# The state-space recurrence regrouped into chunks of four tokens, with its small matrices built on the chip

## The reference

```python
def s5_mixer(h, h0, lam_re, lam_im, log_dt, b_re, b_im, c_re, c_im, d_skip, w_glu):
    lam = lax.complex(lam_re, lam_im); dt = jnp.exp(log_dt)[:, None]
    a_bar = jnp.exp(lam * dt)
    b_bar = ((a_bar - 1.0) / lam)[..., None] * lax.complex(b_re, b_im)
    u = h.reshape(Bt, S, SSM_GROUPS, SSM_P)                # 64 groups of 16 channels
    bu = jnp.einsum('bsgp,gnp->bsgn', u, b_bar)            # 64 complex states a group
    bu = bu.at[:, 0].add(a_bar[None] * h0)
    _, states = lax.associative_scan(combine, (a, bu), axis=1)   # s_t = a s_(t-1) + bu_t
    y = jnp.real(jnp.einsum('bsgn,gpn->bsgp', states, c_mat)) + d_skip * u
    z = y @ w_glu
    return z[..., :D] * jax.nn.sigmoid(z[..., D:]), last_state
```

## Time and profile before

| | us |
|---|---|
| median of three runs | 2583.43 |
| the profiled execution, its time | 2582.37 |
| the profiled execution, its span | 2580.6 |
| TensorE busy | 2400.8 (93%) |
| VectorE busy | 1625.4 (63%) |
| ScalarE busy | 963.7 (37%) |
| GpSimd busy | 802.7 (31%) |

### The profile page before, as it was taken

The page is one execution under the profiler, slowest core; times in us unless marked ns, Lnnn a source line. Parts: engine busy times, 40 slices in busy tenths (PEclk is TensorE's granted clock), DMA queues, the critical chain, the costliest instruction groups (busy, mean ns, idle before and its releaser), DMA issues.

```text
span 2580.6 us, 48876 instructions
## 1 busy us (share of the span) xinstructions
PE 2400.8 (93%) x17574; PEld 2207.2 (86%) x17574; DVE 1625.4 (63%) x3405; ACT 963.7 (37%) x1664; POOL 802.7 (31%) x580
## 2 busy tenths in 40 slices
PE   4689789999999999999968988899999999999998
PEld 1344679999999999999958666699999999999998
DVE  6999736978899733333345442279788996333333
ACT  1122225444444344444423332254444344444443
POOL 0278736790000022222245300268700001222222
PEclk6699999999999999999989988899999999999999
DMA  8555234443333444444453463344433334444443
GB/s 307 185 211 180 78 133 140 164 145 130 123 130 128 151 163 165 169 163 164 167 218 111 175 255 138 125 139 160 142 131 124 129 130 157 163 165 168 163 163 140
DMA packets 105467, 405.81 MB, mean 157 GB/s; under 512 B 12864, under 2 KB 13248, under 8 KB 102176
## 3 DMA queue, kind: packets, MB, share of 16 engines
q1 hardware_dynamic: 98064, 357.74, 39.8%
q10 hardware_dynamic: 7312, 46.93, 4.7%
HBM read 395.48 MB, written 9.14 MB: 157 GB/s over the span
## 4 chain that ended last, share of the span: by engine, by line
PE 62%; issue 17%; DVE 10%; POOL 9%; ACTq 1%; ACT 1%; DMA 0%; POOLq 0%; DVEq 0%
PE ps L1239 11%; PE ps L1231 10%; PE ps L1235 10%; POOL ring_lo L1827 7%; PE ps L1211 6%; PE ps L1210 6%; PE ps L1214 6%; PE ps L1198 5%; DVE big L1548 2%; POOL ring_lo L1834 1%; PE ps L1109 1%; PE ps L1105 1%; PE ps L1106 1%; DVE big L1540 1%; PE ps L706 1%
## 5 line engine op out<-in xcount | busy, mean ns | idle before, releaser
L330 ACT ACTIVATE wt_hi<-ring 128x1024 fp32r<-128x1024 f32 x564 | 593.7, 1053 | 347.7 <-PE ps L1109 209.3
L1748 DVE TENSOR_TENSOR ring_lo<-ring,wt_hi 128x1024 fp32r<-128x1024 f32 x256 | 314.6, 1230 | 492.2 <-ACT wt_hi L330 492.2
L1845 POOL TENSOR_TENSOR split<-big,w_hi 128x288 fp32r<-128x288 f32 x256 | 208.0, 813 | 1201.8 <-PE ps L1214 603.3
L1827 POOL TENSOR_TENSOR ring_lo<-ring,wt_hi 128x1024 fp32r<-128x1024 f32 x112 | 308.0, 2757 | 126.1 <-ACT wt_hi L330 126.1
L1210 PE MATMUL ps<-split,wt_hi 128*128 128x288 f32 x1152 | 328.5, 307 | 0.0
L1211 PE MATMUL ps<-split,wt_hi 128*128 128x288 f32 x1152 | 316.1, 298 | 0.0
L1239 PE MATMUL ps<-w_hi,ring_lo 128*128 128x288 f32 x2048 | 313.1, 295 | 1.5 <-DVE ring_lo L1748 1.5
L1235 PE MATMUL ps<-split,wt_hi 128*128 128x288 f32 x2048 | 313.1, 295 | 0.3
L1231 PE MATMUL ps<-w_hi,wt_hi 128*128 128x288 f32 x2048 | 312.9, 295 | 0.0
L1239 PEld LDWEIGHTS ps<-w_hi,ring_lo 128*128 128x128 f32 x2048 | 285.4, 188 | 1.9 <-DVE ring_lo L1748 1.9
L1235 PEld LDWEIGHTS ps<-split,wt_hi 128*128 128x128 f32 x2048 | 285.4, 188 | 0.8 <-POOL split L1845 0.8
(11 more groups left out here) (291 smaller groups left out, 3602.4 us busy)
## 6 DMA issues: line engine op xcount, KB each, us to landing
ring<-in_stream SPq DMA_DIRECT2D x680, 512.0 KB, 3.2
big<-in_kc ACTq DMA_DIRECT2D x8, 1792.0 KB, 13.3
big<-in_vc ACTq DMA_DIRECT2D x8, 1792.0 KB, 8.1
out_qk<-big ACTq DMA_DIRECT2D x1, 3456.0 KB, 16.4
x_keep<-xT ACTq DMA_DIRECT2D x2, 1152.0 KB, 5.1
xT<-x_keep ACTq DMA_DIRECT2D x2, 1152.0 KB, 5.7
out_v<-big ACTq DMA_DIRECT2D x1, 1536.0 KB, 18.5
xT<-in_xT ACTq DMA_DIRECT2D x1, 1152.0 KB, 9.5
```

Source lines behind the costliest of these rows:

```text
L330: nc.scalar.activation(wt_hi[:, n % 2], ring[:, n % RING], ACT.Copy).then_inc(S["hi_ready"], 1)
L1748: TT(ring_lo[:, s], ring[:, s], wt_hi[:, s % 2].bitcast(F32), ALU.subtract)\
L1827: TT(ring_lo[:, s], ring[:, s], wt_hi[:, s % 2].bitcast(F32), ALU.subtract)\
L1845: TT(w_lo[:, s % 2], W[:, bass.ds(4 * i + s, 1), :].rearrange("p a t -> p (a t)"), w_hi[:, s % 2].bitcast(F32), ALU.subtract).then_inc(S[" ...
```

## The change: what it does

The recurrence works on chunks of four tokens. A chunk's 4 tokens x 32 channels fill the 128 partitions (`u5`), the prompt gives 64 chunks and each sample one, 72 columns. With T a 128 x 128 block-triangular matrix for a pair of groups, y = T u + C' x, where x is the state ahead of the chunk; x comes from a scan over 64 chunks in place of 256 tokens, with a to the fourth power as its factor. Eight rounds ("batches") of four pairs of groups take the place of the 32 rounds.

The parts:

- **New matrices.** TensorE turns B (32 products of 64 x 64) and spreads d (16 of 32 x 8) before the first projection tile. VectorE computes the powers of a, fills the matrices `btp` and `cw`, and then makes `c_sel` (before: first of all). GpSimd clears `btp` and `cw`. After block 2 TensorE does 64 transposes (`turn_b`), copied out by ScalarE; after `mean_square` in block 3 it does 256 products for T (`toeplitz`), masked by VectorE. The tables have 64 columns in place of 288, and the block matrices of b_bar (L636, L1781) are gone.
- **Chunk copies.** After the modulation ScalarE (18) and VectorE (14) copy `hT` into `u5`.
- **A batch.** TensorE: `s5_in(b)` with 8 products of 72 columns, two steps of layer 1's projection (two pairs), and `s5_out(b-1)` with 4 + 8 products. ScalarE writes y back with four copies a batch (`y_out`). Four steps of the projection stand ahead of the batches, sixteen among them, four behind.

```diff
+            for z, raw in enumerate((sbre, sbim)):
+                for c in range(NC):
+                    for g in range(2):
+                        mm(ps[64 * g:64 * g + 64, z, 64 * c:64 * c + 64], raw[:, 64 * c:64 * c + 64], pick, ...)
...
+            def turn_b(n):
+                if n >= 4:
+                    pe.wait_ge(S["s5_trc"], n - 3)
+                for a in range(4):
+                    ins = nc.tensor.transpose(ps[:, TURN_BANK[n % 4], 128 * a:128 * a + 128], btp[:, z, 4 * i + a, :], ident)
+            def toeplitz(i):
+                if i >= 4:
+                    pe.wait_ge(S["s5_tc"], i - 3)
+                for a in range(4):
+                    for z in range(2):
+                        for r in range(4):
+                            ins = mm(ps[32 * r:32 * r + 32, TURN_BANK[i % 4], 128 * a:128 * a + 128],
+                                     btp[:, z, k, 96:128], cw(z, k, -r), ...)
...
             for nb in range(6):
...
+                if nb == 2:
+                    pe.wait_ge(S["s5_b0c"], 1)
+                    pe.wait_ge(S["s5_bp"], 1)
+                    for n in range(16):
+                        turn_b(n)
                 if nb == 3:
                     mean_square(0)
+                    pe.wait_ge(S["s5_trc"], 16)
+                    pe.wait_ge(S["s5_cp"], 1)
+                    for i in range(8):
+                        toeplitz(i)
...
-            for k in range(PAIRS + 3):
-                if k < PAIRS:
-                    s5_in(k)
-                if k >= 3:
-                    s5_out(k - 3)
-                if 2 <= k < 26:
-                    ...
-                    ada_two(1, nb, c, 7)
+            def s5_in(b):
+                if b >= 2:
+                    pe.wait_ge(S["s5_rot"], b - 1)
+                    pe.wait_ge(S["s5_zl"], b - 1)
+                for c in range(4):
+                    for z in range(2):
+                        ins = mm(bu5(b)[:, z, c, :], bw[:, z, k, :], u5[:, 4 * half + c, q, :], ...)
+            def s5_out(b):
+                for c in range(4):
+                    mm(y[:, c, :], tw[:, 4 * (4 * half + c) + q, :], u5[:, 4 * half + c, q, :], ...)
+                pe.wait_ge(S["s5_xo"], b + 1)
+                for c in range(4):
+                    for z in range(2):
+                        ins = mm(y[:, c, :], cw(z, 4 * (4 * half + c) + q, 1), x5[b % 2][:, z, c, :], ...)
+            for i in range(4):
+                ada_step(i)
+            for b in range(8):
+                s5_in(b)
+                for i in range(4 + 2 * b, 6 + 2 * b):
+                    ada_step(i)
+                if b:
+                    s5_out(b - 1)
+            s5_out(7)
+            for i in range(20, 24):
+                ada_step(i)
+            ada_turn(1, 5)
...
     (ScalarE)
+                act.wait_ge(S["s5_rot"], b + 1)
+                nc.scalar.activation(zl[:, :, 4 * half:4 * half + 4, q, :], bu5(b)[:, :, :, CH:CW], ACT.Copy)
+                if b >= 2:
+                    y_out(b - 2)
+                if b == 6:
+                    y_high(0)
+                if b % 2 == 0:
+                    ada_row(act, 1, b // 2, 7)
+            y_out(6)
+            y_out(7)
+            y_high(1)
+            for nb in (4, 5):
+                ada_row(act, 1, nb, 7)
+            act.wait_ge(S["ada_turned"], 12)
             high(act, GLU)
...
     (GpSimd)
+                TT(x[:, 0, :, 1:CH], m[:, 0, :, 0:CH - 1], m[:, 3, :, 0:CH - 1], ALU.subtract)
+                TT(x[:, 1, :, 1:CH], m[:, 1, :, 0:CH - 1], m[:, 2, :, 0:CH - 1], ALU.add)
+                TT(last[:, 0], ...)
+                TT(last[:, 1], ...).then_inc(S["s5_xo"], 1)
```

More of the change, by code:

```diff
@@ L648, in _ @@
[L648 to L658, removed]
@@ L659, in _, with to_chunks @@
[L659 to L661 removed]
+            def to_chunks(half, n0, n1):
+                for n in range(n0, n1):
+                    ra, q = slice(32 * (n // 4), 32 * (n // 4) + 32), n % 4
+                    ins = nc.scalar.activation(u5[ra, 4 * half:4 * half + 4, q, :], chunks(half, n), ACT.Copy)
+                ins.then_inc(S["s5_ua"], 1)
@@ L1375, in _ @@
             nc.vector.memset(cwide_t, 0.0).then_inc(S["c_zero"], 1)
-            v.wait_ge(S["in_setup"], 16 * 7)
+            nc.vector.memset(jmask, 1.0)
+            nc.vector.memset(tmask, 0.0)
+            own(nc.vector.memset(cw_t[:, :, 0:96], 0.0))
+            own.settle()
+            nc.vector.memset(jmask[:, 0:1], 0.0)
+            for r in range(4):
+                ins = nc.vector.memset(tmask[32 * r:32 * r + 32, 32 * r:128], 1.0)
+            own(ins)
             def square_x(q, dst):
@@ L1380, in square_x @@
                     TT(dst[:, m], xT[:, m], xT[:, m], ALU.mult).then_inc(S["sq_ready"], 1)
-            own.settle()
-            square_x(0, hT)
-            for z in range(2):
-                ins = TT(csel[:, z], ident[:, 32 * z:32 * z + ROWS], ident[:, 32 * z + 64:32 * z + 64 + ROWS], ALU.add)
-            ins.then_inc(S["c_sel"], 1)
-            v.wait_ge(S["in_s5"], 16 * 6)
+            v.wait_ge(S["in_s5"], 16 * 7)
             v.wait_ge(S["s5_trig"], 1)
@@ new lines, in _ @@
+            nc.vector.memset(bbar[:, 0, 0, 0:1], 0.0).then_inc(S["s5_bp"], 1)
+            v.wait_ge(S["in_setup"], 16 * 5)
+            square_x(0, hT)
+            for z in range(2):
+                ins = TT(csel[:, z], ident[:, 32 * z:32 * z + ROWS], ident[:, 32 * z + 64:32 * z + 64 + ROWS], ALU.add)
+            ins.then_inc(S["c_sel"], 1)
+            v.wait_ge(S["s5_cc"], 1)
+            own(TS(pn, pw, -1.0, None, ALU.mult))
+            own.settle()
+            pc = [[w[:, z].rearrange("p q k -> p k q").unsqueeze(3).broadcast_to([P, PAIRS, 4, 16]) for z in range(2)]
+                  for w in (pw, pn)]
@@ new lines, in scan @@
+                TT(planes(m[:, 0:2]), twice(tcos, b), planes(z), ALU.mult)
+                TT(planes(m[:, 2:4]), twice(tsin, b), planes(z), ALU.mult).then_inc(S["s5_op"], 1)
+            for b in range(9):
+                if b < 8:
+                    rot_in(b)
+                if b:
+                    scan(b - 1)
+            v.wait_ge(S["s5_zl"], 8)
+            TT(st[:, :, :, 1:], st[:, :, :, 1:], zl.rearrange("p z c q b -> p z (c q) b"), ALU.add).then_inc(S["s5_rm"], 1)
+            v.wait_ge(S["yh_ready"], 2)
@@ L1822, in low_u @@
+            for b in range(9):
+                if b < 8:
+                    z_in(b)
+                if b:
+                    x_out(b - 1)
+            pool.wait_ge(S["yh_ready"], 1)
+            TT(y_lo[:, 0:4], hT[:, 0:4], y_hi[:, 0:4].bitcast(F32), ALU.subtract).then_inc(S["yl_ready"], 1)
             def low_u(l, j0, j1):
```

516 lines of the change are left out of this document (305 added, 211 removed).

## The result

The changed kernel takes 2604.23 us (median of 4 runs, 2603.10 to 2608.04) against 2582.68 us before (4 runs, 2580.41 to 2583.77). The ratio is 1.0086, 95% interval [1.0073, 1.0098]: slower, by 18.9 to 25.3 us. The prediction was 2597 us with a range of 2561 to 2618; the chance of slower was given as 0.55. The profiled execution took 2603.1 us, 6 more than predicted.

What follows compares the result with a forecast made beforehand. Only the first 290 us could move, with TensorE without slack behind them: the head costs 44.3 us, the middle gains 29.5, so +14.8 on the profiled 2582.4 gives 2597 us, range 2561 to 2618.

Steps and rivals of the forecast that it cites:

- the mixed clock: Main case for the recurrence: odd batches at 11.5 us, even ones at 18.5, program 2597 us; chance 0.45.
- The head: Stretch up to layer 0's last turn: predicted to end at 152.1 us against 107.8, a cost of 44.3 us.
- `c_sel` at 52: In the head: VectorE has the selection matrix ready at 52 us, and TensorE's first turn waits until then.
- the one term of the transposes: In the head, turn_b after block 2: 64 transposes at the half clock, 0.27 us each, 17 us.
- From the last turn to `s5_in(0)`: Between head and recurrence: modulation, then VectorE's four chunk copies; s5_in(0) starts at 163.7 us against 121.4.
- The clock of the recurrence: In the batches: full clock not expected to last through even ones; odd taken at 11.5 us, even at 18.5.
- The two prices of a batch at the half clock: In the recurrence: 13.7 us for an odd batch and 20.6 for an even one.
- half clock throughout: Rival for the recurrence: batches of 13.7 and 20.6 us, +30.3 us at the GLU, 2613 us; chance 0.14.
- the rise behind 121.4: Recurrence of the kernel before: TensorE began at 1.2 GHz and its clock rose behind unbroken work; cited against the half clock.
- The signs named for the profile: Profile after: among others, batches alternating between about 11 and 18 us, granted clock 0.6 to 0.8 between 165 and 300.
- The series: In each batch: rotation, scan, rotation back, x_out take 6.5 us after s5_in(b); then eight C and eight s5_in(b+1) products.
- The tail: Behind the batches: last scans, s5_out(7), y_out, y_high, ada_row, four pairs, two turns, first GLU tile: 34 us.

Runs made afterwards that it cites:

- e1: The changed kernel with the two operations that fill csel moved from behind the squares to the front of VectorE's program: 2590.62 us.
- e7: The changed kernel with each of the 64 transposes of turn_b done twice into the same place: 2608.9 us.
- e8: The changed kernel with csel and ada_row early, s5_in one batch ahead, block 4's ada_row ahead of y_out(6), chunk copies split 8 and 8: 2542.54 us.
- e9: The kernel of e8 with six unread 128x64 products added ahead of every second pair of a batch: 2586.52 us.
- e10: The changed kernel with unread wide products (224 moving columns, four at a time) added in TensorE's waits for ada_row and x_out: 2589.33 us.
- e3: The changed kernel with s5_in(b+1) moved to the front of batch b on TensorE, other engines unchanged: 2575.08 us.

## Why the prediction came out as it did

The sign and its mechanism were right: the head costs more than the recurrence gives back. At the first low product +14.8 us were forecast and +24.9 came, and behind that figure errors of both signs partly cancel. The stated range, 2561 to 2618, ran from faster to slower, so that the time lies in it says little; the case that came nearest is the mixed clock (0.45), whose own range of 2588 to 2606 holds 2604.2 near its top. That it does is partly luck, as the terms show.

**The head: 37.7 us, not 44.3.** The B products were over at 20.9, less than 4 us where I gave 5 to 14, and hide as said. `c_sel` at 52 was right (52.36), with VectorE as the releaser, and e1 shows the wait of 12.5 us to be worth its full length (13.6 in the time). The pairs up to `turn_b` ended at 75.8, not 73.0. `turn_b` was sized at 17 us and took 8.4, for two reasons. The half clock was carried on from the stretch ahead, but it rose 2.3 us into the group. And a transpose costs 0.213 us at the half clock, not 0.27, and 0.109 at the full one: the 1.6/12 of L1181 holds the ends of two short groups. Half clock throughout would have been 13.7 us and the full one 7.0, so the price makes 3.3 of the error and the clock 5.3; that 8.4 fits the lower end given, 8.5, is chance. `toeplitz` took 14.2 against 15.9, the rest 30.0 against 29.5. What failed is the one term of the transposes, by 8.6 us; the other terms add up to +2.0.

The choice of 17 leaned on the Trainium skill (TensorE: Matmul & The Clock Gate, Part 4: PE-mode transpose), by which transposes don't count as activity for the clock. The trace of after has 0.73 from 76 to 80 us and 1.00 from 80 to 84, and e7 has 1.00 through its second 64. The measurement decides: here they held the clock.

**From the last turn to `s5_in(0)`: 15.3 us, 11.6 predicted.** The modulation was right (both halves 9.6 us, from 145.5 to 155.1; the first one is ready at 152.0). But ScalarE's twelve copies for the first half take 0.72 us each. I had looked at VectorE's four only (0.42 us each, as it came out) and had laid L366's 0.393 under the copies; L366 is a Gelu on 128 partitions. They end at 160.7, and that is when `s5_in(0)` starts. e8 takes 1.7 us of it away. From `s5_in(0)` to `s5_in(1)` it took 13.8 us for 15.8, with the turn at the full clock. The same price stands in `y_out`, 2.73 us for 1.6, and so in the wait of even batches, 4.9 to 5.8 us for 4.1.

**The clock of the recurrence: the step that was off.** The two prices of a batch at the half clock, 13.7 and 20.6 us, were right in sum; within an even one the wait was 0.8 us longer and the products as much shorter. Measured, `s5_in(1)` to `s5_in(7)`: 13.6, 20.7, 13.6, 17.7, 11.8, 21.6 (the last with `y_high`). What was wrong was the choice between the levels, 11.5 and 18.5. The sum is 99.0 us against 91.2 (+7.8), nearly the 104.1 of the half clock throughout. I had argued from the rise behind 121.4, that two pairs would lift the clock; but what ran there were products of 288 columns. Now three quarters of TensorE's products have 9 or 72 columns (48 of 64 in two batches). e9 shows that such work keeps the half clock for 88 us without any wait, and e10 that wide work in the same waits lifts it to 0.74 and gives 15 us. So the rival "half clock throughout" was nearer than its 0.14, and the row that spoke for it, a turn and two pairs 7.1 us without a break at the half clock, told more than the waits by which I chose. The signs named for the profile say the same: batches of 11 and 18 us and a clock of 0.6 to 0.8 were called right, and from 165 to 300 us it was 0.58. What exactly the clock answers to stays open.

**The series: right.** From the end of `s5_in(b)` to the first C product it took 6.5 us as computed wherever TensorE waited in the batches (208.9 to 215.4), with 8 + 8 products behind it and `x_out` at 1.8 us, and e3 shows its worth, 29 us, in one line of order. The prediction saw the series and priced it, but treated it as given, and it didn't say that the scan in it is the batch before's. In the last batch, where the scan of batch 7 ran beside it, `x_out(6)` took the 3.3 us of the contended price.

**The tail: 41.2 us, not 34.** From `s5_in(7)` to the low product. Up to the last C product it was 16.9 us for 13, with the wait of 4.00 us for that slow `x_out(6)` and the C products at the half clock; the wait for `ada_row` 4.60 for 3.4, behind `y_out(7)` (2.69) and `y_high` (1.16); four pairs and two turns with the stream's waits 15.7 for 14; the first GLU tile 4.0 for 3.5.

In sum, against the forecast: `s5_in(1)` ended 4.9 us earlier (174.6 for 179.5), batches +7.8, tail +7.2, which is +10.1; 4 us come back behind. The rows tie 1.2 to the GLU. It is 24.1 us at 1590 us and 20.7 at 1640: 3.4 come back in one place, where the execution before had a wait of 1.61 us for a transfer and a stretch of half clock (1600.2 to 1603.6 us) that after's had not; 64 products took 17.45 and 15.76 us there. Before, then after:
```profile
1594.14 1.74 PE L830 MATMUL ps<-big 128*32 128x128 f32 x56 [1.61 <-DMA big<-in_vc]
...
1599.13 17.45 PE L1001 MATMUL ps<-big,ring 128*128 128x288 f32 x64 [0.58 <-issue]
```
```profile
1614.97 3.37 PE L912 MATMUL ps<-big 128*32 128x128 f32 x112
...
1621.59 15.76 PE L1083 MATMUL ps<-big,ring 128*128 128x288 f32 x64 [0.58 <-issue]
```
The instructions are the same there, so this may be chance of the two executions; no run shows it. That leaves the 6 us between 2597 and 2603.1.

## What to carry to other kernels

A regrouping that trades long products for many short ones should be priced with TensorE at the half clock first, and only be given the full one where a row shows such short products running at it. When an engine's order puts step b's input behind step b-1's output, look whether a double buffer already allows it one step ahead: here one moved call was worth more than the whole difference between the two kernels. Look at the same time for such an order on a second engine: VectorE's rotation of b ahead of its scan of b-1 and TensorE's output of b-1 ahead of its input of b+1 together made the series. And a two-operation constant that a fast engine waits for belongs at the front of the slow engine's program, whatever it seems to belong to.

## What the hardware showed that was not expected

- TensorE was busy 88.0 of 88.0 us at a granted clock of 0.50 (e9), in products of 9, 64 and 72 moving columns with pairs between. In 128-column transposes it stayed at 1.00 for 13 us (e7). The Trainium skill (TensorE: Matmul & The Clock Gate, Part 1) has the gate watch how busy the engine has been; these rows don't fit a reading of busy as "not idle" in the profile's sense. What exactly counts was not settled.
- Fillers can slow a kernel by more than their own length: e9's 20 us of small products cost 44 in the median and 34 in the profiled execution.
- A ScalarE copy of 288 columns on 32 partitions takes 0.68 to 0.72 us where a Gelu of 288 contiguous columns on 128 partitions takes 0.393; the strides (every fourth column) differ as well, and which of the two costs was not taken apart.
